# SSD layer of a four-layer decoder step: decays of rows from the segment banks, state updates by row groups, time steps by column groups, reordered projections

## What is computed

```
proj = x @ w_in                       # z (2048) | xs (2048) | B (8x128) | C (8x128) | dt (32)
xbc  = silu(causal_conv(xbc, conv_state, conv_w, conv_b))
dt   = softplus(dt_raw + dt_bias);  a = -exp(a_log)
acs  = cumsum(dt * a)                 # within a chunk of 128 rows (8 rows of a sample sequence)
y_diag = einsum(C.B, exp(acs_l - acs_s) where s <= l, x*dt)
states = sum_s B_s * exp(acs_end - acs_s) * (x*dt)_s ;  s_final = s * exp(acs_end) + states
y_off  = exp(acs_l) * (C_l . state at the chunk's start)
y = (y_diag + y_off + d_skip * xs) * silu(z);  rms over groups of 256;  y @ w_out
```

## Time and profile before

| | |
|---|---|
| median of 3 runs | 2367.73 us (2364.25 to 2370.97) |
| the profiled execution | 2374.75 us |
| its span | 2373.0 us |
| TensorE busy / mean granted clock | 92% of the span / 0.914 |
| VectorE, ScalarE, GpSimd busy | 54%, 41%, 53% |

### The profile page before, as it was taken

The page is one execution under the profiler, slowest core; times in us unless marked ns, Lnnn a source line. Parts: engine busy times, 40 slices in busy tenths (PEclk is TensorE's granted clock), DMA queues, the critical chain, the costliest instruction groups (busy, mean ns, idle before and its releaser), DMA issues.

```text
span 2373.0 us, 37830 instructions
## 1 busy us (share of the span) xinstructions
PE 2192.3 (92%) x14852; PEld 1993.0 (84%) x14852; DVE 1271.1 (54%) x2173; ACT 982.0 (41%) x1585; POOL 1253.2 (53%) x1565
## 2 busy tenths in 40 slices
PE   6898999879999999899989999999999889989997
PEld 5888997678898987798779898998899779889976
DVE  5798344156666666354146666555324338982342
ACT  3677443323334333243343333332243347764322
POOL 4798882333344443274345444444486049988802
PEclk8999999978889887799988999888799999999998
DMA  3444566233433332267331333334366524445760
GB/s 114 141 125 129 192 204 224 72 111 86 119 111 111 111 110 92 64 206 260 131 98 63 109 109 120 112 120 129 110 222 203 176 86 137 129 130 171 254 202 25
DMA packets 329760, 321.35 MB, mean 135 GB/s; under 512 B 21512, under 2 KB 311216, under 8 KB 329584
## 3 DMA queue, kind: packets, MB, share of 16 engines
q1 hardware_dynamic: 328720, 318.60, 42.1%
q10 hardware_dynamic: 864, 0.34, 0.1%
HBM read 289.27 MB, written 29.61 MB: 134 GB/s over the span
## 4 chain that ended last, share of the span: by engine, by line
PE 71%; DVE 16%; ACT 5%; DMA 3%; issue 2%; POOL 2%; SPq 1%; ACTq 0%; DVEq 0%
PE ps L678 11%; PE ps L679 10%; PE ps L683 10%; PE ps L1218 4%; PE ps L688 3%; PE ps L668 3%; PE ps L669 3%; PE ps L670 3%; PE ps L1064 2%; DVE work L2081 2%; PE ps L1085 2%; PE ps L1263 2%; PE ps L946 2%; PE ps L955 2%; DVE work L1931 2%
## 5 line engine op out<-in xcount | busy, mean ns | idle before, releaser
L1413 POOL TENSOR_TENSOR wl<-raw,wh 128x256 fp32r<-128x256 f32 x1536 | 1248.6, 851 | 1084.7 <-ACT wh L1436 1083.4
L678 PE MATMUL ps<-Hh,wh 128*128 128x320 f32 (+1 forms) x1536 | 485.3, 332 | 59.9 <-DVE Hl L1977 26.3
L1436 ACT ACTIVATE wh<-raw 128x1024 fp32r<-128x1024 f32 (+1 forms) x400 | 399.7, 1020 | 324.0 <-DMA raw<-hg_w_in 80.0
L679 PE MATMUL ps<-Hl,wh 128*128 128x320 f32 (+1 forms) x1536 | 469.8, 322 | 0.0
L678 PEld LDWEIGHTS ps<-Hh,wh 128*128 128x128 f32 x1536 | 313.2, 204 | 79.5 <-issue 45.8
L679 PEld LDWEIGHTS ps<-Hl,wh 128*128 128x128 f32 x1536 | 314.4, 205 | 1.3
L683 PE MATMUL ps<-Hh,wl 128*128 128x320 f32 (+1 forms) x1536 | 255.5, 309 | 4.3 <-POOL wl L1413 4.3
L1931 DVE TENSOR_SCALAR work<-ps 128x512 f32<-128x512 f32 (+9 forms) x248 | 116.0, 485 | 251.7 <-PE ps L1229 42.7
L683 PEld LDWEIGHTS ps<-Hh,wl 128*128 128x128 f32 x1536 | 233.4, 193 | 6.4 <-POOL wl L1413 6.4
L668 PE MATMUL ps<-Oh,wh 128*128 128x320 f32 x512 | 170.9, 334 | 9.5 <-POOL wl L1413 5.4
L669 PE MATMUL ps<-Ol,wh 128*128 128x320 f32 x512 | 166.7, 326 | 0.0
(11 more groups left out here) (406 smaller groups left out, 4066.7 us busy)
## 6 DMA issues: line engine op xcount, KB each, us to landing
raw<-rg_w_in SPq DMA_DIRECT2D x128, 256.0 KB, 3.6
raw<-hg_w_in SPq DMA_DIRECT2D x128, 256.0 KB, 5.1
raw<-ssd_w_in SPq DMA_DIRECT2D x96, 256.0 KB, 3.7
work<-cache_mem_k SPq DMA_DIRECT2D x40, 512.0 KB, 5.8
raw<-rg_w_out SPq DMA_DIRECT2D x64, 256.0 KB, 3.5
raw<-x_w_k SPq DMA_DIRECT2D x64, 256.0 KB, 3.5
raw<-x_w_v SPq DMA_DIRECT2D x64, 256.0 KB, 5.3
raw<-x_w_q SPq DMA_DIRECT2D x64, 256.0 KB, 3.6
```

Source lines behind the costliest of these rows:

```text
L678: pe.matmul(ps[:, bank, 0:n], high(half, k), mh[:, k, 0:n], start=(k == 0), stop=False)
L679: pe.matmul(ps[:, bank, 0:n], high(half, k), ml[:, k, 0:n], start=False, stop=False)
L1413: ins = pool.tensor_tensor(out, src, wh[:, n % HALVES, r:r + 2].bitcast(F32), ALU.subtract)
L1436: act.activation(wh[:, n % HALVES, 0:rows], raw[:, slot, 0:rows, half * P:(half + 1) * P], ACT.Copy).then_inc(hi_ready, 1)
```

## The change

- The twelve products into bank 7 go, with ScalarE's one exponential of them. ScalarE now reads the sums of the rows from the segment banks 5 and 6 themselves (four exponentials of half the partitions, two for the prompt's second chunk and two for the samples), between its other exponentials; fading takes the last row of each sample sequence from there. The transposed states go to banks 4, 7, 5, 6.
- `gains` contracts over the 32 rows that can be non-zero: rows 64 to 95 for the first half of the sequences, 96 to 127 for the second. The four products alternate between two row groups of the array.
- `time_steps` becomes 8 fp32 products with the 32 columns of the weights as the stationary operand and 320 moving columns, into four column groups of bank 4 (k and k + 4 share one), placed before `take_x(0, 0)`. ScalarE copies the rows out, and `turn_steps`, three products with a selecting matrix `sd_sel` (sums of pieces of the identity, made by VectorE), adds the four groups and transposes. The high and low halves of these weights are no longer made.
- z of group 0 goes to banks 6 and 7 and waits for nothing; the waits of `take_bc(1, .)` become waits for the copies out of banks 0 and 1; `turn(0)` waits for `gate(0)` instead; `take_x(1, 0)` comes before `turn(0)`.
- In every turn TensorE does `outputs(j, 0)` before `take_z(i, 1)`, and VectorE does `gate(i)` between `outputs(j, 0)` and `outputs(j, 1)`. VectorE copies the history of group 0 before its time steps.

```diff
-        wdth, wdtl = sb("wdth", [P, KD, 32], F32R), sb("wdtl", [P, KD, 32], F32R)
...
+        def z_of(i):
+            return ps[:, 0:2, 0:NT] if i else ps[:, 6:8, 0:NT]
+
+
+        ST_BANK = (4, 7, 5, 6)
...
-        sd_eo, sd_s0 = c(2, 200), c(2, NB, P)
+        sd_eo, sd_s0 = c(2, 192), c(2, NB, P)
...
+        sd_dth, sd_sel = sd_yo2[:, 0, :], smallc[:, 448:480]
...
                 def time_steps():
-                    pe.wait_ge(*past("sd_wdt", 1))
+                    pe.wait_ge(*past("in_wdt", 16))
+
+                    for k in range(KD):
+                        r = 32 * (k % 4)
+                        mm = pe.matmul(ps[r:r + 32, 4, 0:NT], wdt[:, k, :], Y[:, k, :], start=(k < 4), stop=(k >= 4))
+                    mm.then_inc(S("sd_dth_full"), 1)
+
+                def turn_steps():
+                    pe.wait_ge(*past("sd_sel", 1))
+                    pe.wait_ge(*past("sd_dth_read", 1))
                     for T in range(3):
                         t0 = (0, P, NT - P)[T]
-                        for k in range(KD):
-                            for n, (x, w) in enumerate(((Hh, wdth), (Hh, wdtl), (Hl, wdth))):
-                                mm = pe.matmul(ps[:, 4, 32 * T:32 * T + 32], x[:, k, t0:t0 + P], w[:, k, :],
-                                               start=(k == 0 and n == 0), stop=(k == KD - 1 and n == 2))
+                        mm = pe.matmul(ps[:, 4, NT + 32 * T:NT + 32 * T + 32], sd_dth[:, t0:t0 + P], sd_sel, start=True, stop=True)
                     mm.then_inc(S("sd_dt_full"), 1)
...
                 def take_bc(i, half):
                     if half == 0:
-                        if i:
+                        if i == 1:
+                            pe.wait_ge(*past("sd_in_ready", 1))
+                        elif i:
                             pe.wait_ge(*past("sd_z_read", i))
                         project(0, 0)
                         return
+                    if i == 1:
+                        pe.wait_ge(*past("sd_ht_read", 1))
                     pe.wait_ge(*past("sd_hist_in", i * 48 + 48))
                     project(1, 1)
...
                 def take_z(i, half):
+                    if i == 0:
+                        project(6 + half, half)
+                        return
                     pe.wait_ge(*past("sd_in_ready", i + 1))
                     if half:
                         pe.wait_ge(*past("sd_ht_read", i + 1))
...
                         pe.wait_ge(*past("sd_sums_read", 1))
+                        pe.wait_ge(*past("sd_z_read", 1))
...
                     mm.then_inc(S("sd_seg2_full"), 1)
-                    for t in range(2):
-                        c = 200 * t
-                        for n in range(2):
-                            out, h = ps[64 * n:64 * n + 64, 7], 2 * t + n
-                            pe.matmul(out[:, c:c + P], dta(1, h, 64), upper[:], start=True, stop=True)
-                            pe.matmul(out[:, c + P:c + 192], dta(2, h, 64, sm), s_causal[sm], start=True, stop=True)
-                            mm = pe.matmul(out[:, c + 192:c + 200], dta(2, h, 64, sm), s_block[sm], start=True, stop=True)
-                    mm.then_inc(S("sd_eo_full"), 1)
 
                 def turn_states(j):
-                    for n, read in enumerate(("sd_seg0_ready", "sd_seg1_ready", "sd_seg2_ready", "sd_eo_read")):
+                    for n, reads in enumerate((("sd_seg0_ready",), (), ("sd_seg1_ready", "sd_eo1_read"), ("sd_seg2_ready", "sd_eo2_read"))):
                         if n % 2 == 0:
                             pe.wait_ge(*past(f"sd_s0_in{n // 2}", j * 16 + 16))
-                        pe.wait_ge(*past(read, j + 1))
+                        for read in reads:
+                            pe.wait_ge(*past(read, j + 1))
                         for b in range(4):
-                            mm = pe.transpose(ps[:, 4 + n, b * P:(b + 1) * P], sd_s0[:, n // 2, 4 * (n % 2) + b, :], ident[:])
+                            mm = pe.transpose(ps[:, ST_BANK[n], b * P:(b + 1) * P], sd_s0[:, n // 2, 4 * (n % 2) + b, :], ident[:])
                         mm.then_inc(S(f"sd_st{n}_full"), 1)
...
                 def outputs(j, t):
-                    pe.wait_ge(*past(f"sd_st{1 + t}_read", j + 1))
                     if t == 0:
                         pe.wait_ge(*past("sd_m_ready", j + 1))
                         pe.wait_ge(*past("sd_st3_read", j + 1))
...
-                        xw = sd_xw[sm, 2, 2 * t:2 * t + 2, :].rearrange("p h c -> p (h c)")
-                        pe.matmul(ps[:, bank, :], xw, sd_bm[sm, 4 * half:4 * half + 4, :].rearrange("p b n -> p (b n)"), start=True, stop=True).then_inc(S(f"sd_sn{n}_full"), 1)
+                        rows = slice(64 + 32 * half, 96 + 32 * half)
+                        xw = sd_xw[rows, 2, 2 * t:2 * t + 2, :].rearrange("p h c -> p (h c)")
+                        pe.matmul(ps[:, bank, :], xw, sd_bm[rows, 4 * half:4 * half + 4, :].rearrange("p b n -> p (b n)"), start=True, stop=True).then_inc(S(f"sd_sn{n}_full"), 1)
...
                         take_bc(i, 1)
+                    if i == 0:
+                        time_steps()
+                    if i == 1:
+                        take_x(i, 0)
                     if j >= 0:
                         turn(j)
-                    if projects:
+                    if projects and i != 1:
                         take_x(i, 0)
-                    else:
+                    elif not projects:
                         take_out(2, 1, 0, 9)
                     if j >= 0:
                         decays(j)
                     if i == 0:
-                        time_steps()
+                        turn_steps()
                     if projects:
                         take_x(i, 1)
                     else:
...
                     if j >= 0:
                         prompt_states(j)
                         turn_pack(j)
+                    if j >= 0:
+                        outputs(j, 0)
                     if projects:
                         take_z(i, 1)
                     if j >= 0:
-                        outputs(j, 0)
                         outputs(j, 1)
...
-                act.wait_ge(*past("in_wdt", 16))
-                act.activation(wdth[:], wdt[:], ACT.Copy).then_inc(S("sd_wdt_high"), 1)
+                def rows_of_steps():
+                    act.wait_ge(*past("sd_dth_full", 1))
+                    act.activation(sd_dth, ps[:, 4, 0:NT], ACT.Copy).then_inc(S("sd_dth_read"), 1)
...
-                    act.activation(sd_z[i % 2], ps[:, 0:2, 0:NT], ACT.Sigmoid).then_inc(S("sd_z_sig"), 1)
+                    act.activation(sd_z[i % 2], z_of(i), ACT.Sigmoid).then_inc(S("sd_z_sig"), 1)
...
                 def exps(j):
+
+                    def of_sums(bank, w, at, n):
+                        rows = slice(64 * n, 64 * n + 64)
+                        sums = ps[rows, bank, 0:4 * w].rearrange("p (t n c) -> p t n c", t=2, n=2)[:, :, n, :]
+                        return act.activation(sd_eo[rows, :, at:at + w], sums, ACT.Exp)
+
                     for T in range(3):
                         act.wait_ge(*past(f"sd_seg{T}_ready", j + 1))
+                        if T:
+                            steps.did(of_sums(4 + T, (P, 64)[T - 1], (0, P)[T - 1], 0))
+                            of_sums(4 + T, (P, 64)[T - 1], (0, P)[T - 1], 1).then_inc(S(f"sd_eo{T}_read"), 1)
                         rows, w = (slice(0, P), P) if T < 2 else (slice(64, P), 64)
                         act.activation(sd_e[rows, T, :, 0:w], sd_e[rows, T, :, 0:w], ACT.Exp).then_inc(S(f"sd_exp{T}"), 1)
-                    act.wait_ge(*past("sd_eo_full", j + 1))
-                    act.activation(sd_eo, ps[:, 7, 0:400].rearrange("p (t c) -> p t c", t=2), ACT.Exp).then_inc(S("sd_eo_read"), 1)
 
                 def states(j):
                     for n in range(4):
                         act.wait_ge(*past(f"sd_st{n}_full", j + 1))
-                        act.activation(sd_st[:, n // 2, 4 * (n % 2):4 * (n % 2) + 4, :], ps[:, 4 + n, :].rearrange("p (b c) -> p b c", b=4), ACT.Copy).then_inc(S(f"sd_st{n}_read"), 1)
+                        act.activation(sd_st[:, n // 2, 4 * (n % 2):4 * (n % 2) + 4, :], ps[:, ST_BANK[n], :].rearrange("p (b c) -> p b c", b=4), ACT.Copy).then_inc(S(f"sd_st{n}_read"), 1)
...
                     if i == 0:
+                        rows_of_steps()
                         ahead(u + 3)
                         steps_of_time()
...
-                wait("sd_wdt_high", 1)
-                tt(wdtl[:], wdt, wdth[:].bitcast(F32), SUB).then_inc(S("sd_wdt"), 1)
+                did(tt(sd_sel, ident[:, 0:32], ident[:, 32:64], ADD))
+                for r in (64, 96):
+                    sync()
+                    ins = tt(sd_sel, sd_sel, ident[:, r:r + 32], ADD)
+                    if r == 64:
+                        did(ins)
+                    else:
...
+                def history(i):
+                    wait("sd_ht_full", i + 1)
```

(27 more changed lines are left out.)

7 lines of the change are left out of this document (4 added, 3 removed).

## The result

The changed kernel takes 2290.94 us (median of 4 runs, 2283.92 to 2295.38) against 2369.35 us (4 runs) for the kernel before on the same chip: ratio 0.9669, interval 0.9642 to 0.9695, 78 us less. A second set gives 2286.71 us and the same ratio, 0.9669 (0.9644 to 0.9695). The profiled execution is the 2283.92 us one, the fastest of its set.

The account below looks back on a forecast made before the run. TensorE, busy in 92% of the span and partly at 1.2 GHz, was taken as the bound; 27.5 us up to turn 1's end plus later turns' savings made 87.7, giving a median of 2280 us, range 2260 to 2309.

Parts of the forecast that it names:

- Turns: SSD stage, turn to turn: turn 2 saves 9.6 us, turns 3 to 6 36.8, turn 7 7.8.
- Clock: Sparse outputs and gains lower TensorE's clock; remaining loss 3.8 us in turns 1, 2 and 7, 1.5 in turns 3 to 6.
- Sums for bank 7: Removing these products takes 2.75 us off TensorE's path in each turn.
- Gains: The four gains products in two row groups overlap and take 1.85 us instead of 3.70 at full clock.
- the rival without overlap: Gains products in two row groups don't run at once: 18 us less saved, 2298 us; chance 0.17.
- Time steps: Group 0: new time-step products take 1.4 us, turning products 0.7; sums there at 495.0 instead of 505.3.
- The step that failed: Group 0: VectorE's softplus takes 7.5 us, plus about 2.2 for ScalarE's late exponential, done at 504.7.
- The last turn: Saves 6 us in all: 2.75 for bank 7 and an estimated 3 as VectorE adds gains as they come.
- The expected wait of about 1.3 us before the fourth gains product: Turns 1, 2 and 7: TensorE waits for VectorE to free the bank, as nothing lies between outputs(j,1) and gains.
- VectorE as the bound: Nearly all VectorE convolution steps are slow, lengthening convolution and fading by about 5 us a turn: 2306 us; chance 0.12.
- Clock never falls: Every sparse run is too short to lower TensorE's clock, so 17 us more go: 2263 us; chance 0.12.
- Slower: Clock falls in outputs(j,0) and stays at 1.2 GHz until the next turn: 2417 us; chance 0.02.

Follow-up runs that it names:

- the order alone: Kernel before with only outputs(j,0) moved ahead of the second half of z and VectorE's gate behind it: 2350.54 us, ratio 0.9932.
- the restored version: Changed kernel with the twelve products of the sums for bank 7, one exponential and the old state banks back: 2321.30 us, ratio 0.9825.
- second profile: The changed kernel run once more without any edit, as base for the other versions: 2286.71 us, ratio 0.9669 to the kernel before.
- two versions: Changed kernel with gains over all 64 rows (2306.41 us, ratio 0.9751), or all four products over the same 32 rows (2303.16 us, 0.9755).

## Why the prediction was right, and where its terms were off

The forecast was 2280 us within 2260 to 2309; the medians are 2290.9 and 2286.7, and the two profiled executions 2283.9 and 2290.4 against 2287. The sum was 87.7 us, the stage gave 79.6 and 82.4, the medians 78.4: the forecast was 5 to 9 us too good, and that the first profiled execution came within 3 us of its number is the luck of two executions on either side of their medians. Part by part it was 27.5 us up to the end of turn 1 (measured 23.6 and 24.0), 9.6 (10.2 and 10.2), 36.8 (33.0 and 36.1), 7.8 (7.7 and 7.8) and 6 (5.1 and 4.3).

- **Turns.** Turn 1: 42.3 forecast, 42.6 and 41.8 measured; turn 2: 45.1, 44.5; turns 3 to 6: 196.1, 199.9 and 196.8; turn 7: 42.9, 43.0. These steps held.
- **Clock.** The forecast left 17.4 us of loss in turns 1 to 7 of 53.1 and so took 35.7 out; the windows give 106 to 33 us at the low clock, 37 us. The sum was right, but its cause was put too narrowly: "The sparse run was outputs, outputs, gains". Undoing the order gives back 34 us of low clock, undoing the gains 14, the bank-7 sums 20; the order alone took 54 out. The order has the largest share, but all three sparse stretches lowered the clock, and the bank-7 sums had no term for it.
- **Sums for bank 7.** 2.75 us a turn was right for the products (678.51 to 681.26 in the restored version). The part is worth 31.1 us, 9 more than its term, by the clock.
- **Gains.** Taken at 1.85, "because column groups overlap fully": measured 2.0 on the timeline's scale, as 3.7 was. The 18 us of the rival without overlap is what the part is worth, 18.0 in the stage, though by other shares: it allowed 3 us for the clock, and the 14 us of low-clock time cost 7. The Trainium skill, TensorE: Matmul & The Clock Gate, section Part 3, reports 3.07 times for four row groups; the estimate of 2.4 us worked out from it was too high for the two of this case, which gave 1.86 times (3.7 over 1.99 us).
- **Time steps.** 16 records in 1.28 us and the turning products in 0.75, for 1.4 and 0.7; they were done at 494.1, for 495.0.

```profile
488.55 1.28 PE L825 MATMUL ps<-work 128*32 128x320 f32 x16
493.38 0.75 PE L833 MATMUL ps<-smallc,work 128*128 128x32 f32 x6
```

- **The step that failed: "VectorE's softplus takes from 505.3 to 512.8, 7.5 us".** From the sums to the step sizes it was 17.4 us, where the forecast had 9.7 with the late exponential. Its row was taken beside an idle GpSimd, and the change moved it to where GpSimd works. The step sizes came at 511.5 instead of 504.7, and TensorE waited for them:

```profile
511.67 0.38 PE L840 MATMUL ps<-work,upper 128*128 128x32 f32 x2 [3.38 <-DVE work L2215]
```

The convolution, which the forecast took at its old length beside GpSimd, ran without it: from the step sizes to the end of `activate` it was 10.7 us (522.2 less 511.5) for 16.3, so 5.6 came back; turn(0) followed TensorE's units at 524.0, 3.0 us behind the forecast. No wait for `f_ready` was left there.
- **The last turn.** 6 us forecast, 5.1 and 4.3 measured: the wait for VectorE's `turned` grew from 3.2 to 6.9 us, since ScalarE's split ahead of it waited for its weight block until 863.2. In SyncE's queue that block's load stands behind the last state load, and was issued at 856.0, 2.0 us after turn(7), where before it was issued at 927.9, 1.2 us ahead of it. The forecast looked at state loads, not at what stands behind them.
- **The expected wait of about 1.3 us before the fourth gains product** is there in turns 1 and 7 (1.2 and 1.3 us in the first profile) and not in turn 2; in the second profile it is in turn 7 alone (1.3).
- **Rivals.** No overlap: excluded by two versions. VectorE as the bound: not at turns 1 to 7 (the twelve accumulating steps of a convolution took 8.8 us there, for 9.3 before), though not far away, as the waits in turns 1 and 7 show. Clock never falls: no; it stays up only in some of turns 3 to 6. Slower: no, the z unit and `take_out` did hold the clock.

Single parts, undone one at a time, are worth 18.0 + 12.9 + 31.1 + 7.3 + 8.6 = 77.9 us of the stage against 81.0 for all: they nearly add up, the clock's share among them.

## What to carry to other kernels

When a stretch of work is moved, take its instructions' durations from where they will run: here short VectorE steps nearly tripled beside GpSimd's subtractions. Count a removed sparse stretch at more than its own length where the granted clock falls behind it (2.75 us were 3.9 here). For a load, ask what stands ahead of it in its queue. And alternate row groups for products over few rows: it is the other group, not fewer rows, that halves them.

## What the runs showed that was not expected

Two-record fp32 products of 512 columns in two row groups overlap nearly fully: 8 records of 0.6 us in 2.0 us, against 3.7 in one group. A turn whose sparse stretches are 3.8, 3.8 and 1.9 us, each between dense units, can stay at 1.00 for its 48.5 us (turn 4 of the second profile), and its neighbours in the same profile do not (0.97 over 49.9 and 50.0 us); in the first profile turn 5 is at 0.93 over 51.6. What decides between them was not found. The time behind the stage varies by 23 us between profiles of kernels that are the same there (1350 to 1373), more than any of the small parts measured here. The two longest (1367 and 1373) are those of the kernel before and of that kernel with the new order; whether that is more than chance is not shown, but the medians, 78.4 us apart for 79.6 and 82.4 in the stage, speak against it.
